# Input projections of an attention layer by Strassen's seven products

## The reference

```python
q_k_v_g = rms_norm(x, norm_w) @ w_in          # 544x2048 @ 2048x8192, 16 heads of 128 columns in each of q, k, v, g
q, k = rms_norm(q, q_w), rms_norm(k, k_w)     # per head
z = q @ k.T * HEAD_DIM ** -0.5                # strictly causal, with the past frames' keys
log_one_minus = where(earlier, log_sigmoid(-z), 0)
between = reverse_cumsum(log_one_minus) - log_one_minus
w = where(earlier, exp(log_sigmoid(z) + between), 0)
x = x + ((w @ v) * silu(g)) @ w_out           # 2048x2048
```

## Time and profile before

| | |
|---|---|
| median of three executions | 2336.28 us |
| profiled execution, its span | 2341.37 us, 2339.6 us |
| TensorE busy | 2299.0 us (98%), granted clock 0.995 of full speed |
| VectorE, ScalarE, GpSimd busy | 1294.5 us (55%), 1025.7 us (44%), 90.6 us (4%) |
| matmuls at line 498 | 15360 of 17977, 80% of the chain that ended last |
| from HBM, to HBM | 186.41 MB, 24.38 MB |

### The profile page before, as it was taken

The page is one execution under the profiler, slowest core; times in us unless marked ns, Lnnn a source line. Parts: engine busy times, 40 slices in busy tenths (PEclk is TensorE's granted clock), DMA queues, the critical chain, the costliest instruction groups (busy, mean ns, idle before and its releaser), DMA issues.

```text
span 2339.6 us, 45158 instructions
## 1 busy us (share of the span) xinstructions
PE 2299.0 (98%) x17977; PEld 2276.2 (97%) x17977; DVE 1294.5 (55%) x2214; ACT 1025.7 (44%) x1402; POOL 90.6 (4%) x87
## 2 busy tenths in 40 slices
PE   7999999999999999999999999999999999998999
PEld 6999999999999999899999999999999999997999
DVE  6444444444444444533267777777777777777221
ACT  5444444444444444532254444444444444444221
POOL 5000000000000000311000000000000000003000
PEclk9999999999999999999999999999999999998999
DMA  7333222332222232245532222222222222212542
GB/s 239 98 86 86 86 86 86 86 86 86 86 86 86 86 86 86 67 124 144 140 92 77 75 75 75 75 75 75 75 75 75 75 75 75 75 48 69 140 119 79
DMA packets 388086, 211.26 MB, mean 90 GB/s; under 512 B 9091, under 2 KB 378294, under 8 KB 388022
## 3 DMA queue, kind: packets, MB, share of 16 engines
q1 hardware_dynamic: 340182, 181.19, 27.2%
q10 hardware_dynamic: 47872, 29.64, 4.2%
HBM read 186.41 MB, written 24.38 MB: 90 GB/s over the span
## 4 chain that ended last, share of the span: by engine, by line
PE 94%; DVE 2%; ACT 1%; issue 0%; ACTq 0%; DVEq 0%
PE psum L498 80%; PE psum L621 3%; PE psum L489 2%; PE psum L596 1%; PE psum L544 1%; PE psum L570 1%; PE psum L580 1%; ACT work L805 1%; PE psum L667 1%; ACT act_hi L805 1%; PE psum L646 1%; PE psum L669 0%; PE psum L526 0%; PE psum L525 0%; PE psum L550 0%
## 5 line engine op out<-in xcount | busy, mean ns | idle before, releaser
L498 PE MATMUL psum<-act_hi,w_hi 128*128 128x272 f32 x5120 | 1080.7, 292 | 12.4 <-DVE act_lo L1177 5.3
L498 PE MATMUL psum<-act_hi,w_lo 128*128 128x272 f32 x5120 | 1062.0, 289 | 0.0
L498 PE MATMUL psum<-act_lo,w_hi 128*128 128x272 f32 x5120 | 1059.0, 288 | 0.0
L1168 DVE TENSOR_TENSOR w_lo<-w_raw,w_hi 128x1024 fp32r<-128x1024 f32 x320 | 401.8, 1256 | 777.5 <-ACT w_hi L805 777.2
L498 PEld LDWEIGHTS psum<-act_hi,w_hi 128*128 128x128 f32 x5120 | 805.4, 189 | 15.6 <-DVE act_lo L1177 4.4
L498 PEld LDWEIGHTS psum<-act_lo,w_hi 128*128 128x128 f32 x5120 | 807.1, 189 | 0.0
L498 PEld LDWEIGHTS psum<-act_hi,w_lo 128*128 128x128 f32 x5120 | 802.9, 189 | 0.0
L805 ACT ACTIVATE w_hi<-w_raw 128x1024 fp32r<-128x1024 f32 x320 | 338.0, 1057 | 603.7 <-PE psum L498 560.3
L805 ACT ACTIVATE work<-work 128x544 f32<-128x544 f32 (+6 forms) x368 | 256.5, 726 | 337.5 <-DVE work L1311 191.1
L805 ACT ACTIVATE work<-psum 128x512 f32<-128x512 f32 (+5 forms) x256 | 111.4, 483 | 142.7 <-PE psum L489 115.4
L474 POOL TENSOR_TENSOR act_lo<-full,act_hi 128x544 fp32r<-128x544 f32 x24 | 37.1, 1546 | 1868.2 <-DVE act_lo L1177 1843.7
(11 more groups left out here) (218 smaller groups left out, 1716.9 us busy)
## 6 DMA issues: line engine op xcount, KB each, us to landing
w_raw<-in_w_in SPq DMA_DIRECT2D x256, 512.0 KB, 4.0
w_raw<-in_w_out SPq DMA_DIRECT2D x64, 512.0 KB, 6.6
out<-work ACTq DMA_DIRECT2D x48, 256.0 KB, 2.4
x_residual<-work ACTq DMA_DIRECT2D x32, 272.0 KB, 3.8
work<-x_residual SPq DMA_DIRECT2D x32, 272.0 KB, 2.9
full<-in_x_prompt SPq DMA_DIRECT2D x3, 1024.0 KB, 11.1
work<-in_cache_k ACTq DMA_DIRECT2D x16, 128.0 KB, 2.2
work<-in_cache_v ACTq DMA_DIRECT2D x16, 128.0 KB, 4.1
```

What stands on the lines that cost most here:

```text
L498: mm = pe.matmul(acc[par][:, j, :], w[:, slot, k % KH, :], a[:, k, j * HT:(j + 1) * HT], start=(k == 0 and n == 0), stop=(k == KT - 1 and ...
L1168: dve.tensor_tensor(w_lo[:, slot], w_raw[:, slot], w_hi[:, slot].bitcast(F32), ALU.subtract).then_inc(lo_ready, 1)
```

## The change

**Seven products.** For heads 1 to 15 of layer 0 the tiles come in pairs: q with k, gate with v. A pair's weights are a 2x2 matrix of quarters (two tiles by two halves of the channels), the activations another (two halves of the channels by two halves of the positions). The pair's four result quarters come from seven products of a weight combination with an activation combination in place of eight (Strassen's scheme in Winograd's form). A product is 8 x 3 = 24 matmuls of 272 columns; a head has 14 of them.

**Activations.** The four combinations T1 to T4 are made once, ahead of the loop: the 16 blocks of x are read back from DRAM into `full`, scaled by the norm weights, subtracted and split. T2 and T3 stay in `full`; so head outputs no longer fit there. They go to a small buffer, to DRAM (`o_spill`), and come back before the output projection.

**Weights.** Three of a pair's seven weight operands are loaded quarters, four are sums that VectorE makes, each from the one before it (`weight_sum`). A piece is a quarter or a sum; its split is in `piece_hi` and `piece_lo`, into three slots of `w_hi` and `w_lo`, since slot 3 now holds other buffers. The result quarters are combined and scaled by VectorE (`fast_add`), with one copy per pair by ScalarE (`prod_1`).

**Order.** The loop runs four times over three heads, and a fifth time unrolled. Attention's steps are spread over the 14 products: the sums stand behind product 0, the scores behind 3, `att_cumulated` behind 9, `att_mixed` behind 12.

**The last low parts.** At the end of layer 1 VectorE makes all low parts of the output projection's activations (`LAST_REST`); GpSimd's `split_last(1)` is gone.

In the diff the first `fast_turn` is TensorE's, the second ScalarE's, the third VectorE's.

```diff
+            def load_d(q, pair, first=False):
+                sp_eng.wait_ge(lo_ready, 7 if first else q * PRODUCTS + (HEAD_HALVES - PRODUCTS + 6))
+                sp_eng.dma_start(w_raw[:, 2], fast_weights(q, 1, 1, pair)).then_inc(quarter_loaded[2], 16)
...
+            def load_o(m):
+                heads = slice(4 * m, min(4 * m + 4, H - 1))
+                sp_eng.wait_ge(half_done, OUT_BASE[0] - 4)
+                sp_eng.wait_ge(o_stored, 16 * heads.stop)
+                sp_eng.dma_start(full[:, heads, :], o_spill[heads].rearrange("k p t -> p k t")).then_inc(o_back[m], 16)
...
+            def product(i, off):
+                pair, idx = off // PRODUCTS % 2, off % PRODUCTS
+                b_hi, b_lo = FAST_B[idx]
...
+                pe.wait_ge(lo_ready, piece(i, off) + 1)
+                for k in range(KH):
+                    for m, (w, a) in enumerate(((w_hi, b_hi), (w_hi, b_lo), (w_lo, b_hi))):
+                        mm = pe.matmul(bank, w[:, r, k, :], a[:, k, :], start=fresh and k == 0 and m == 0,
+                                       stop=k == KH - 1 and m == 2, skip_group_check=True)
+                mm.then_inc(half_done, 1)
+            def fast_turn(i):
+                for n in range(BODY):
+                    for s in range(HEAD_PIECES):
+                        product(i, n * HEAD_PIECES + s)
+                        if s == 0:
+                            att_sums_and_turns(i * BODY + n)
+                        elif s == 3:
+                            att_scores(i * BODY + n)
+                        elif s == 9:
+                            att_cumulated(i * BODY + n)
+                        elif s == 12:
+                            att_mixed(i * BODY + n)
...
+            def piece_hi(i, off):
+                idx, g, q = off % PRODUCTS, piece(i, off), pair_of(i, off)
+                act.wait_ge(half_done, g - 2)
+                if idx in QUARTER:
+                    act.wait_ge(quarter_loaded[QUARTER[idx]], q * 16 + 16)
+                else:
+                    act.wait_ge(sum_made, q * 4 + SUM[idx])
+                func(w_hi[:, off % 3], raw_of(off), ACT.Copy).then_inc(hi_ready, 1)
...
+            def fast_turn(i):
+                for n in range(BODY):
+                    for s in range(HEAD_PIECES):
+                        off = n * HEAD_PIECES + s
...
+                            piece_hi(i, off + 2)
...
+                        if s == 10:
+                            prod_1(i, off - 3)
+                        att_act(i * BODY + n, s)
+                        if s == 2:
+                            prod_1(i, off - 2)
...
+            def weight_sum(i, off):
+                c, e = chain_raw(par), chain_raw(1 - par)
...
+                    if idx == 3:
+                        ins = dve.tensor_tensor(e, c, w_raw[:, 0], ALU.subtract)
+                    else:
+                        raw = 2 if idx == 2 else 1
+                        dve.wait_ge(quarter_loaded[raw], q * 16 + 16)
+                        ins = dve.tensor_tensor(c, c, w_raw[:, raw], ALU.add)
...
+            def fast_turn(i):
...
+                            piece_lo(i, off + 2)
...
+                        if s in (3, 8):
+                            att_dve(i * BODY + n, s)
+                        if not (last_turn(i) and off + 3 >= BODY_PIECES):
+                            weight_sum(i, off + 3)
+                        if s:
+                            fast_add(i, off - 1)
+                        if s not in (3, 8):
+                            att_dve(i * BODY + n, s)
+                    fast_add(i, off)
```

More of the change, by code:

```diff
@@ L769, in _ @@
                                 half_ready(g0 + par + 2 * (k // KH), t0 + par, k // KH)
[L770 removed]
+                            mm = part(par + 2 * (k // KH), par, [k], w0, l == 0 and par == 1 and k >= KH)
                             if k == KH - 1:
@@ L1069, in _ @@
[L1069 to L1079 removed]
+                    hi(7, 3)
+                    rows_scaled(0)
+                    rows_scaled(1)
@@ new lines, in _ @@
+                    for m in range(4):
+                        func(t1_hi[:, 2 * m:2 * m + 2, :], t1_full[:, 2 * m:2 * m + 2, :], ACT.Copy
+                             ).then_inc(diff_hi_ready, 1)
+                    for m in range(2):
+                        func(T4[0][:, 4 * m:4 * m + 4, :], t4_full[:, 4 * m:4 * m + 4, :], ACT.Copy
+                             ).then_inc(diff_hi_ready, 1)
+                    with act.Fori(0, TURNS - 1) as i:
+                        ch.enter(i, 30)
+                        fast_turn(i)
+                        ch.leave(TURNS - 1)
@@ new lines, in _ @@
+                    fast_turn(TURNS - 1)
+                else:
+                    for u in range(HEAD_HALVES):
+                        split_ahead(l, 0, u)
+                        if u == 2:
+                            rms(1)
+                            load_state(0)
+                        if u >= 5:
+                            rec_next(0, u)
+                    rec_decays(0)
+                    with act.Fori(0, H - 1) as h:
+                        ch.enter(h, 13)
+                        for u in range(HEAD_HALVES):
+                            split_ahead(l, h + 1, u)
@@ L1167, in lo, with piece_lo @@
                 dve.wait_ge(hi_ready, g + 1)
-                dve.tensor_tensor(w_lo[:, slot], w_raw[:, slot], w_hi[:, slot].bitcast(F32), ALU.subtract
+                out = w_lo_first if isinstance(g, int) and g == OUT_BASE[0] + 3 else w_lo[:, slot]
+                dve.tensor_tensor(out, w_raw[:, slot], w_hi[:, slot].bitcast(F32), ALU.subtract
                                   ).then_inc(lo_ready, 1)
+            def piece_lo(i, off):
+                dve.wait_ge(hi_ready, piece(i, off) + 1)
+                dve.tensor_tensor(w_lo[:, off % 3], raw_of(off), w_hi[:, off % 3].bitcast(F32), ALU.subtract
+                                  ).then_inc(lo_ready, 1)
@@ new lines, in fast_add, with done, put @@
+            def fast_add(i, off):
+                pair, idx, q = off // PRODUCTS % 2, off % PRODUCTS, pair_of(i, off)
+                if idx < 2:
+                    return
+                r1, r2 = FAST_TILES[pair]
+                x, w_, y, z = fast_banks(pair)
+                c11, c12, c21, c22 = Y[:, r1, 0:HT], Y[:, r1, HT:T], Y[:, r2, 0:HT], Y[:, r2, HT:T]
+                def done(n):
+                    dve.wait_ge(fast_added, q * EVACS + (EVACS + n))
+                def put(out, a, b, op):
+                    dve.tensor_tensor(out, a, b, op).then_inc(fast_added, 1)
+                dve.wait_ge(half_done, piece(i, off) + 1)
+                if idx == 2:
+                    dve.wait_ge(prod_1_copied, q + 1)
+                    put(c12, y, c11, ALU.add)
+                    done(1)
+                    put(c22, w_, c12, ALU.subtract)
+                elif idx == 3:
+                    done(2)
+                    put(c22, c22, z, ALU.subtract)
+                elif idx == 4:
+                    put(c11, x, rstd_x[:, 0:HT], ALU.mult)
+                elif idx == 5:
+                    put(c21, w_, c12, ALU.subtract)
+                    done(5)
+                    dve.tensor_tensor(Y[:, r2, :], Y[:, r2, :], rstd_x[:], ALU.mult).then_inc(evacuated, 1)
+                else:
+                    put(c12, z, c12, ALU.add)
+                    done(6)
+                    dve.tensor_tensor(c12, c12, rstd_x[:, HT:T], ALU.mult).then_inc(evacuated, 1)
```

547 lines of the change are left out of this document (390 added, 157 removed).

## The result

The changed kernel takes 2488.49 us (median of 4 runs, 2485.89 to 2493.71) beside 2338.29 for the kernel before (2335.47 to 2340.57): a ratio of 1.0646, with a 95% interval of 1.0623 to 1.0668. The prediction was 2411 us, with a range of 2320 to 2465. The direction is right, but the 150 us are twice the 75 that were predicted. The profiled execution has a span of 2484.2 us, 144.6 more than before, and this is the difference taken apart here.

The account below looks back on a forecast made before the run. TensorE was taken as the bound, waiting for nobody in layer 0's fifteen heads. Work saved less waits +22, clock +42, start and ends +11 made +75: 2416 us profiled, 2411 median; range 2320 to 2465.

Parts of the forecast that it names:

- TensorE's own work: Layer 0's fifteen heads: fourteen products a head leave 52.5 us of TensorE work, 6.0 less; 90 us saved in all.
- waits with filling: TensorE's waits before sums, scores and att_cumulated in each head: 2.0, 3.5 and 2.0 us, filling included.
- clock: Layer 0's heads: TensorE's granted clock halves after some waits, 2.8 us a head, +42 us; bounds 0 and 5.8 a head.
- start and ends: Outside the fifteen heads: first sums 14 us later, 2.5 us back at the end, tails nothing; together +11 us.
- VectorE as the bound: Rival: VectorE's 58 instructions a head each wait 0.1 us longer, or a sum takes 1.58 us; 2471 us, chance 0.08.
- Together 1.4 + 1.1 + 0.3 = 2.8 a head, +42 us: Sum of clock losses a head behind the waits before the scores, before att_cumulated and before the sums.
- Scores, 1.4: Behind the 3.5 us wait before the scores: half clock costs 1.4 us a head.
- The third wait, 1.1: Wait before att_cumulated: one in three pays 3.4 us of lost clock, counted as 1.1 us a head.
- The sums, 0.3: Wait before the sums: clock loss counts only as sums lengthen (1 us), the scores' wait swallowing the rest; 0.3 a head.
- The rival in which every wait pays in full: Each of the three waits loses clock in every head, 1.4 + 3.4 + 1.0 us; 2456 us, chance 0.06.
- the wait before the sums, 2.0 a head: TensorE behind product 0 waits for qk_lo: 4.8 us chain, 3.0 covered; 1.8 us, 2.0 with filling.
- on ScalarE's queue, where the high parts wait for TensorE anyway: DMAs costed at nothing, including two more DMA issues standing on ScalarE's queue in a head.

Follow-up runs that it names:

- e8: Changed kernel with VectorE's steps 0, 2, 3, 6 and 8 ahead of the low part, loop written out, GpSimd issuing the output's DMA; 2270.14 us, ratio 0.9702.
- e10: Changed kernel with seven matmuls of 512 columns half filling TensorE's wait before the scores, other waits untouched; 2431.39 us, ratio 1.0381.
- e9: Changed kernel with sp_lo computed twice in a row on VectorE, lengthening the wait before att_cumulated; 2546.71 us, ratio 1.0877.
- e7: Changed kernel with the DMA of a head's output issued by GpSimd instead of ScalarE; 2447.20 us, ratio 1.0451.
- e6: Changed kernel with the loop over turns written out on TensorE, ScalarE, VectorE and the load queue; 2482.63 us, ratio 1.0603.
- e1: Changed kernel with three VectorE attention steps (both qk_lo and sp_lo) ahead of the low part in their step; 2305.18 us, ratio 0.9847.
- e3 to e7: Changed kernel, first three each with one VectorE step ahead of its low part: scores' qk_lo 2387.64, sums' qk_lo 2406.67, sp_lo 2453.01 us; e6, e7 have own lines.

## Why the prediction was wrong

The terms, as predicted and as measured in the profiled execution; e8's 791.39 us stand for TensorE's work without waits at full clock.

| term, 15 heads | predicted | measured | from |
|---|---|---|---|
| TensorE's own work | -90 | -86.5 | 791.39 - 877.92 |
| waits with filling | +112.5 | +137 | 55.9 - 9.7 + 3.0 (for a DMA, before the last sums) + 50.6 - 1.2 (behind the last sums) + 26.1 + 5.5 = 130, and 7 of filling |
| clock | +42 | +83 | 881.91 - 791.39 - 7 |
| start and ends | +11 | +10.5 | 12.5 - 2.0 |
| sum | +75 | +144 | |

**What held.** That taking work away pays only where no wait takes its place; which three instructions would be waited for; the wait before the scores (3.5 with filling predicted, 3.27 and 0.16 measured) and before `att_cumulated` (2.0; 1.72 and 0.16); `att_mixed` without a wait; the weight sums (1.22 us measured, 1.23 taken); the start near 98 us (96.3). VectorE as the bound is out: in e8 it is busy for 680 of 795 us, and TensorE waits for 3.4 in all.

**The step that failed: "Together 1.4 + 1.1 + 0.3 = 2.8 a head, +42 us".** Its mechanism was right and its size half of what came, and none of its three parts was right. *Scores, 1.4:* they lost 2.7 us in themselves (5.83 against 3.13 in e10) and about 1.5 in product 4, some 4.1 in most heads. I had taken the length of the slow stretch behind one other wait (2.88 us, rows 10) as if it were a property of the wait. *The third wait, 1.1:* nothing; at 1.72 us it never lowered the clock, and e9 shows that only its length spared it. *The sums, 0.3:* 1.64 in themselves and about 1 in the products behind, in most heads. The reason given, "the wait for the scores swallows the rest", was wrong by the chain that stood a paragraph above it: that chain starts where product 1 ends (443.57 in the timeline), so slower sums and a slower product 1 move the scores' `qk_lo` as far as they move TensorE. The scores' wait was 3.27 us in heads whose sums ran at full clock, too (the one that ends at 385.51 us).

The rival in which every wait pays in full came closest to the clock, with 87 us, but by errors that cancel: its 3.4 us at the third wait were nothing, its 1.4 at the second were 4.1, its 1.0 at the first 2.6. The Trainium skill (TensorE: Matmul & The Clock Gate, HAM oscillation — how this bites in real kernels) tells of a kernel in which every burst of matmuls behind a wait began at half rate. Here 11 of 15 sums and 14 of 15 scores lost the clock, and no `att_cumulated` behind its 1.7 to 2.0 us. The time of the rival with VectorE as the bound, 2471 us, lies nearest to the measured one by luck: its cause is not there.

**The second miss: the wait before the sums, 2.0 a head.** It was 3.1, and 4.3 to 4.75 in the first head of a turn. The DMA issue that I had let lie "on ScalarE's queue, where the high parts wait for TensorE anyway" waits there for VectorE and costs 1.0 (e7), the loop 0.5 in each head (e6), and the jump back 1.8 behind product 13 and 1.2 to 1.7 more before the sums, three times. In the sum: +22 before the sums (49.2 for 15 x 1.8) and +5.5 behind product 13, less 2 in the other two waits, some 25 us.

The range fell short because both terms were off at once: with the clock at its upper bound the time is 2411 + 15 x 3.0 = 2456 us, inside; for 25 us of waiting on top there was no room.

**What cancelled.** The layer's tail was not free: the outputs that come back cost a wait of 5.2 us for GpSimd's rows. But `att_cumulated` waits for nothing there now (1.9 before), and from the last sums to the block that waits for the tail's last rows it is only 1.0 us longer (1108.32 to 1151.74, before 961.73 to 1004.12); the same stretch of layer 1's tail is 3.0 shorter (45.69 us, 48.64 before).

## What to carry over

Before work is taken from a saturated engine, follow each queue that its helpers stand in: here the gain of 86 us was hidden by three steps that were ready and stood behind one that wasn't, and putting them first turned +6.5% into -1.5% (`e1`); two more steps moved, the loop written out and GpSimd's issue made it -3.0% (`e8`). An idle stretch of TensorE can cost more than its length (here some 4 us of clock behind 3.3 us before the scores, none behind 1.7), so a wait of 3 us is worth removing or filling with useless matmuls; fill it to see what the clock alone costs. When several terms come from one or two rows of other places, give the range room for more than one of them to be off: here the clock's upper bound of 5.8 us a head was inside, 5.5 came, and with it a longer wait.

## What the runs showed of the chip

In nine of these runs (the changed kernel and e1, e3 to e7, e9, e10) I counted TensorE's waits before the sums, the scores and `att_cumulated`, from the first to the last sums, and looked at the clock in the 10 us behind each. It was at half for some of them after 1 of 105 waits of 1.5 to 1.8 us, 6 of 14 of 1.8 to 2.3, 21 of 31 of 2.3 to 2.9, 31 of 40 of 2.9 to 3.2, and 108 of 114 of 3.2 to 3.7. So in these runs a longer wait lost the clock more often, but length alone did not decide it: in the changed kernel sums behind the same 3.08 us of waiting ran at 1.00 in three heads:

```profile
371.09:372.98 1.89, 1.89 (x14) 1.71 (x14) 0.81 (x1) 0.00 (x0) 0.00 (x0) 1.00 0.86 245
```

and the scores of these heads then lost 3.1 instead of 4.1 us. A jump back in a loop of 42 products stopped TensorE for 1.8 to 2.0 us, three of three times; written out, none was left. What sets which of two equal waits loses the clock was not settled.
